# Three edits to a one-core fp32 transformer pass: order of the first loads, the pool stage's halves one tile later, and one masked product per scan step

## The reference

```python
for layer in range(DEPTH):
    f = swiglu(rms_norm(h, g[0]), ffn_w_gate[layer, 0], ffn_w_up[layer, 0], ffn_w_down[layer, 0])
    h = h + 0.5 * rms_norm(f, g[1])
    hm = rms_norm(h, g[2])
    if layer < N_A_LAYERS:
        mix = pool_mixer(hm, ...)      # u = h @ w_in; windowed mean of u minus u; group matmul; w_out
    else:
        mix = dilated_mixer(hm, ...)
    h = h + rms_norm(mix, g[3])
    ...                                # second swiglu of the layer
# second block, per layer: HGRN2 scan (both directions), global, differential and window attention
S_t = diag(f_t) S_{t-1} + k_t^T v_t ;  o_t = q_t S_t      # gla_chunk_scan, per head, 64 x 64 state
```

## Time and profile before

| | |
|---|---|
| median of 3 runs | 3438.83 us (3436.82 to 3443.32) |
| the profiled execution | 3444.33 us, its span 3442.5 us |
| instructions | 55261 |
| PE busy | 3204.3 us, 93% of the span |
| DVE / ACT / POOL busy | 43% / 34% / 40% |
| mean granted clock of TensorE | 0.959 |

### The profile page before, as it was taken

How to read it: one execution, slowest core, us unless ns; L and a number is a source line. 1 busy time by engine, 2 the same in 40 slices (tenths; PEclk the granted TensorE clock), 3 DMA queues, 4 the chain that set the end, 5 groups by cost and what they waited for, 6 DMA issues and landing times.

```text
span 3442.5 us, 55261 instructions
## 1 busy us (share of the span) xinstructions
PE 3204.3 (93%) x20656; PEld 2418.0 (70%) x20656; DVE 1473.6 (43%) x3123; ACT 1156.0 (34%) x1979; POOL 1381.4 (40%) x2212
## 2 busy tenths in 40 slices
PE   6999999999999999999999999888989888789888
PEld 5888777787787786777688787666666666556555
DVE  3232454132632235444422236664564345664654
ACT  3222333222421223111322235443434334445444
POOL 3555464454554453333355463331431123323323
PEclk9999999999999999999999999888989999989989
DMA  3222222424334332111133432000000112001011
GB/s 130 97 97 98 86 86 78 139 98 141 106 103 135 133 109 69 56 62 61 57 111 126 140 105 86 31 16 25 32 26 33 61 43 74 26 26 38 32 44 62
DMA packets 74362, 264.71 MB, mean 77 GB/s; under 512 B 7856, under 2 KB 9136, under 8 KB 73904
## 3 DMA queue, kind: packets, MB, share of 16 engines
q1 hardware_dynamic: 67104, 242.25, 21.0%
q10 hardware_dynamic: 7056, 19.69, 1.5%
HBM read 252.47 MB, written 7.34 MB: 75 GB/s over the span
## 4 chain that ended last, share of the span: by engine, by line
PE 82%; DVE 10%; ACT 3%; issue 3%; POOL 0%; DMA 0%; ACTq 0%; DVEq 0%; POOLq 0%
PE ps L1414 28%; PE ps L1443 17%; PE ps L1419 14%; PE ps L1407 3%; PE ps L1937 3%; PE ps L1960 2%; PE ps L1910 2%; PE ps L1517 1%; PE ps L1804 1%; DVE tb L2627 1%; PE ps L1743 1%; PE ps L1990 1%; PE ps L1498 1%; DVE work L2430 1%; PE ps L1824 1%
## 5 line engine op out<-in xcount | busy, mean ns | idle before, releaser
L923 POOL TENSOR_TENSOR wl<-raw,wh 128x256 fp32r<-128x256 f32 x1640 | 1209.9, 769 | 1879.0 <-ACT wh L1020 1248.9
L1042 ACT ACTIVATE wh<-raw 128x1024 fp32r<-128x1024 f32 x224 | 237.6, 1061 | 976.3 <-PE ps L1419 842.6
L1414 PE MATMUL ps<-xh,wh 128*128 128x512 f32 x1392 | 542.7, 390 | 1.7 <-ACT wh L1020 1.7
L1414 PE MATMUL ps<-xl,wh 128*128 128x512 f32 x1392 | 541.6, 389 | 0.0
L1419 PE MATMUL ps<-xh,wl 128*128 128x512 f32 x1392 | 344.3, 389 | 1.2 <-POOL wl L923 1.0
L1020 ACT ACTIVATE wh<-raw 128x1024 fp32r<-128x1024 f32 x186 | 196.7, 1058 | 429.5 <-PE ps L1443 250.7
L1414 PEld LDWEIGHTS ps<-xh,wh 128*128 128x128 f32 x1392 | 261.3, 188 | 59.9 <-ACT wh L1020 3.3
L1419 PEld LDWEIGHTS ps<-xh,wl 128*128 128x128 f32 x1392 | 261.0, 188 | 56.7 <-POOL wl L923 2.7
L1414 PEld LDWEIGHTS ps<-xl,wh 128*128 128x128 f32 x1392 | 261.3, 188 | 53.9
L1414 PE MATMUL ps<-ah,wh 128*128 128x512 f32 x748 | 296.5, 396 | 0.5 <-DVE al L2239 0.5
L1443 PE MATMUL ps<-xh,wh 128*128 128x512 f32 x856 | 278.3, 389 | 19.0 <-issue 7.6
(11 more groups left out here) (374 smaller groups left out, 4934.9 us busy)
## 6 DMA issues: line engine op xcount, KB each, us to landing
raw<-wts_dram SPq DMA_DIRECT2D x458, 512.0 KB, 3.5
spilled_dram<-hc ACTq DMA_DIRECT2D x1, 3072.0 KB, 8.7
hc<-spilled_dram ACTq DMA_DIRECT2D x1, 3072.0 KB, 10.1
tb<-tab_dram ACTq DMA_DIRECT2D x5, 512.0 KB, 3.7
hc<-x_dram ACTq DMA_DIRECT2D x8, 256.0 KB, 9.4
spilled_dram<-hc ACTq DMA_DIRECT2D x1, 2048.0 KB, 7.3
hc<-spilled_dram ACTq DMA_DIRECT2D x1, 2048.0 KB, 8.3
out_dram<-hc SPq DMA_DIRECT2D x8, 256.0 KB, 2.1
```

The source lines that it names most:

```text
L923: ins = pool.tensor_tensor(wl[:, n % SPLIT, piece], raw[:, LOADED[n] % RAW, piece], wh[:, n % SPLIT, piece].bitcast(F32), ALU.subtract)
L1042: act.activation(wh[:, n % SPLIT, :], raw[:, at % RAW, :], ACT.Copy).then_inc(hi_done, 1)
L1414: pe.matmul(out_, wh[:, s, k * P:(k + 1) * P], x_(k, at), start=first, stop=False)
```

## The change

**Opening.** SP now issues the loads in this order: weight tile 0, `x` piece 0, weight tile 1, `x` pieces 2 to 7, weight tiles 2 and 3, constants, masks, levels, context. ACT issues the parameters and `x` piece 1. Each piece of `x` has its own semaphore. The matrix of ones is made by DVE instead of being loaded. PE begins tile 0 when tile 0 has its remainder, and waits for that of tile 1 where tile 1 begins. PE's wait for the constants and for Silu of `cc` stands behind the first two tiles; ACT computes that Silu behind the first gate's Silu; DVE copies the masks before its first gate tile.

**Pool stage.** ACT rounds, and POOL subtracts, the mean of tile n-1 in the step of tile n, and those of the last two tiles both in the step of tile 7 (`pool_parts_after`).

**Scan.** The masks of the near and the far products are one table of 320 columns, and `take` is one product over 2 x 320 columns, the sum and the key copy. The three copies and the clearing of `far` are gone. The state of both heads lies in the same 64 columns, so that `update` has one instruction for it in place of two.

```diff
-NLEV = 2 * NLOW * BLK
+NSCAN = NLOW * BLK + P
+NLEV = 2 * NSCAN
...
-    c["ones"] = np.ones((P, P))
...
-    levels = np.stack([np.stack(low, 1), np.stack(back, 1)], 1).reshape(P, -1).astype(np.float32)
+    far = np.zeros((P, P))
+    for l, s0, q0 in ((6, 0, 64), (5, 0, 32), (5, 64, 96)):
+        far[s0:s0 + (1 << l), q0:q0 + (1 << l)] = 1.0
+    ways = [np.concatenate([np.stack(v, 1).reshape(P, -1), f], 1) for v, f in ((low, far), (back, far.T))]
+    levels = np.concatenate(ways, 1).astype(np.float32)
...
-        const_in, cond_in = sem("const_in"), sem("cond_in")
+        gains_in, ones_ready, const_in, cond_in = sem("gains_in"), sem("ones_ready"), sem("const_in"), sem("cond_in")
+        x_in = [sem(f"x_in{k}") for k in range(KC)]
...
-        far = area(SX + 240, 2 * P).rearrange("p (h t) -> p h t", h=2)
-        lowp = area(SX + 240 + 2 * P, 2 * NLOW * BLK).rearrange("p (h l t) -> p h l t", h=2, l=NLOW)
+        scanned = area(SX + 240, 2 * NSCAN).rearrange("p (h n) -> p h n", h=2)
+        far = scanned[:, :, NLOW * BLK:]
+        lowp = scanned[:, :, 0:NLOW * BLK].rearrange("p h (l t) -> p h t l", l=NLOW)
...
+        def pool_parts_after(number):
+            ins = [m for what, m in POOL_TILES if what == "in"]
+            last = len(ins) - 1
+            return ins[last - 1:] if number == last else ins[number - 1:number] if 0 < number < last else []
...
-            for n in range(RAW):
+            def first_raw(n):
                 sp.dma_start(raw[:, n, :], wts[n * P:(n + 1) * P, :]).then_inc(raw_in[n], 16)
+            def first_x(k):
+                sp.dma_start(hc[:, k, 0:SEQ], x[k * P:(k + 1) * P, :]).then_inc(x_in[k], 16)
+            first_raw(0)
+            first_x(0)
+            first_raw(1)
+            for k in range(2, KC):
+                first_x(k)
+            first_raw(2)
+            first_raw(3)
+            for dst, src in ((cn[:, :], con), (area(0, NMASK), masks), (area(NMASK, NLEV), levels)):
+                sp.dma_start(dst, src).then_inc(const_in, 16)
+            sp.dma_start(hc[:, :, SEQ:TOK], ctx_in).then_inc(cond_in, 16)
...
-                    late = []
-                    for what, m in POOL_TILES:
+                    def part_low(k):
+                        pool.wait_ge(part_hi, c.take("part") + 1)
+                        pool.tensor_tensor(alk(k), tt[:, k % 2, :], ahk(k).bitcast(F32), ALU.subtract).then_inc(a_ready, 1)
+                    for number in range(len(POOL_TILES)):
...
-                        for k in late:
-                            pool.wait_ge(part_hi, c.take("part") + 1)
-                            pool.tensor_tensor(alk(k), tt[:, k % 2, :], ahk(k).bitcast(F32), ALU.subtract).then_inc(a_ready, 1)
-                        late = [m] if what == "in" else []
+                        for k in pool_parts_after(number):
+                            part_low(k)
...
+                    if (name, *at) == ("ffn", 0, 0):
+                        act.wait_ge(x_in[k], 16)
+                        if k == 0:
+                            act.wait_ge(gains_in, 16)
...
+                        if (layer, i) == (0, 0) and number == 0 and j == 0:
+                            give(act.activation(col("cc", 0, 2 * KC), col("cc", 0, 2 * KC), ACT.Silu), a2p, "a2p")
...
+                def part_high(k):
+                    act.wait_ge(part_ready, c.take("part") + 1)
+                    act.activation(ahk(k), tt[:, k % 2, :], ACT.Copy).then_inc(part_hi, 1)
...
-                    if what == "in":
-                        act.wait_ge(part_ready, c.take("part") + 1)
-                        act.activation(ahk(m), tt[:, m % 2, :], ACT.Copy).then_inc(part_hi, 1)
-                    else:
+                    for k in pool_parts_after(number):
+                        part_high(k)
+                    if what == "group":
...
-            for dst, src in ((cn[:], con), (pr[:], par), (area(0, NMASK), masks), (area(NMASK, NLEV), levels)):
-                act.dma_start(dst, src).then_inc(const_in, 16)
-            for k in range(KC):
-                act.dma_start(hc[:, k, 0:SEQ], x[k * P:(k + 1) * P, :]).then_inc(const_in, 16)
-            act.dma_start(hc[:, :, SEQ:TOK], ctx_in).then_inc(cond_in, 16)
-            act.wait_ge(const_in, CONST_LOADS * 16)
-            give(act.activation(col("cc", 0, 2 * KC), col("cc", 0, 2 * KC), ACT.Silu), a2p, "a2p")
+            act.dma_start(pr[:], par).then_inc(gains_in, 16)
+            act.dma_start(hc[:, 1, 0:SEQ], x[P:2 * P, :]).then_inc(x_in[1], 16)
...
-                pe.wait_ge(lo_done, n0 + 2)
+                pe.wait_ge(lo_done, n0 + 1)
...
+                    if j == 1 and k == 0:
+                        pe.wait_ge(lo_done, n0 + 2)
...
+                if (layer, i) == (0, 0):
+                    pe.wait_ge(const_in, CONST_LOADS * 16)
+                    get(a2p, "a2p")
...
-                        pe.matmul(out_banks[:, h, :], qi[s % 2][r, :], state[r, h * HEAD:(h + 1) * HEAD], start=True, stop=False, skip_group_check=True)
+                        pe.matmul(out_banks[:, h, :], qi[s % 2][r, :], state[r, :], start=True, stop=False, skip_group_check=True)
...
-            pe.wait_ge(const_in, CONST_LOADS * 16)
-            get(a2p, "a2p")
+            pe.wait_ge(ones_ready, 1)
...
+                    dve.wait_ge(const_in, CONST_LOADS * 16)
+                    own(dve.tensor_copy(mk[:, :], area(0, NMASK)))
+                    own(dve.tensor_copy(lev.rearrange("p a n -> p (a n)"), area(NMASK, NLEV)))
...
-                    pv = ps[:, 6:8, 0:NLOW * BLK].rearrange("p h (l t) -> p h l t", l=NLOW)
-                    own(dve.tensor_tensor(lowp, pv, lev[:, way].unsqueeze(1).to_broadcast([P, 2, NLOW, BLK]), ALU.mult))
-                    dve.tensor_reduce(lows, lowp.rearrange("p h l t -> p h t l"), AX.X, ALU.add).then_inc(near_ready, 1)
-                    both = ps[:, 6:8, NLOW * BLK:NLOW * BLK + P]
-                    for rows, cols, l in far_products(way):
-                        ins = dve.tensor_copy(far[rows, :, cols], both[rows, :, cols])
-                    ins.then_inc(far_ready, 1)
+                    dve.tensor_tensor(scanned, ps[:, 6:8, 0:NSCAN], lev[:, way].unsqueeze(1).to_broadcast([P, 2, NSCAN]), ALU.mult).then_inc(far_ready, 1)
+                    dve.wait_ge(far_ready, n + 1)
+                    dve.tensor_reduce(lows, lowp, AX.X, ALU.add).then_inc(near_ready, 1)
...
-                for h in range(2):
-                    r = slice(HEAD * h, HEAD * (h + 1))
-                    sh = state[r, h * HEAD:(h + 1) * HEAD]
-                    ins = dve.scalar_tensor_tensor(sh, sh, sd[r, s % 4:s % 4 + 1], state_bank[r, h * HEAD:(h + 1) * HEAD], ALU.mult, ALU.add)
-                ins.then_inc(state_ready, 1)
+                dve.scalar_tensor_tensor(state, state, sd[:, s % 4:s % 4 + 1], state_bank, ALU.mult, ALU.add).then_inc(state_ready, 1)
...
-                    own(dve.memset(far, 0.0))
...
-            dve.wait_ge(const_in, CONST_LOADS * 16)
-            own(dve.tensor_copy(mk[:, :], area(0, NMASK)))
-            own(dve.tensor_copy(lev.rearrange("p a l t -> p (a l t)"), area(NMASK, NLEV)))
...
-            own(dve.tensor_copy(ones_r[:, :], ones))
-            for layer in range(DEPTH):
-                for i in (1, 5):
-                    g = col("norm", (layer * 6 + i) * KC, KC)
-                    own(dve.tensor_scalar(g, g, 0.5, None, ALU.mult))
+            own(dve.memset(sq[:, 0, 0:P], 1.0))
+            dve.tensor_copy(ones_r[:, :], sq[:, 0, 0:P]).then_inc(ones_ready, 1)
+            dve.wait_ge(ones_ready, 1)
...
+            dve.wait_ge(gains_in, 16)
+            for layer in range(DEPTH):
+                for i in (1, 5):
+                    g = col("norm", (layer * 6 + i) * KC, KC)
+                    own(dve.tensor_scalar(g, g, 0.5, None, ALU.mult))
...
```

More of the change, by code:

```diff
@@ L564 @@
 WORK = 9728
-CONST_LOADS = 4 + KC
+CONST_LOADS = 3
 MAGIC = 1.5 * 2.0 ** 23
```

13 lines of the change are left out of this document (7 added, 6 removed).

## The result

The changed kernel takes 3394.45 us (median of 4 runs, 3393.35 to 3396.05), beside 3440.92 (4 runs, 3436.82 to 3443.32) for the kernel before in the same job: a ratio of 0.9867, 95% interval 0.9849 to 0.9884, or 46 us. The profiled execution took 3396.05, against 3444.33: 48.3 us less.

What follows compares the result with a forecast made beforehand. PE, busy 93% of the span, was taken as the bound. Terms -15.1, -3.5, -13 and -2 sum to -33.6: profiled 3444.3 to 3410.7, or 3405 us against the median; own range 3396 to 3413, 8 in 10 within 3392 to 3419.

Steps and rivals of the forecast that it cites:

- the rival in which all of DVE's saved time counts: Whole kernel: nearly all 31 us saved on DVE lie on the path and the clock gains too, 3390; chance 0.14.
- the clock: Mixers: shorter waits leave fewer PE stretches at 1.2 GHz, taken as -2 us, between 0 and -8.
- Term 1: Opening: PE's first product at about 10 us instead of 26.5, partly given back; -15.1 us, bounds -12.5 to -16.5.
- The stall: After the first two tiles: PE waits for ACT's Silu of `cc`, +1.3 us.
- Term 2: Pool stage: earlier rounding and an earlier last `al` shorten PE's wait; -3.5 us, bounds -1 to -5.
- DVE's chain: Pool stage: DVE's means slow by 0.9 us as POOL's work moves forward, leaving the last `al` 3.9 us earlier.
- Term 3: Mixers' scan: shorter `take`, one update instruction and no clearing of `far`; -13 us, bounds -5 to -20.
- 28 x 0.41 = 11.5: Scan: `take` gets 0.41 us shorter on average, and PE waits for it 28 times; -11.5 us.
- The first rival: Scan: PE waits for ACT or its own order instead, so the scan gives 5 us, not 15: 3415; chance 0.17.
- The state's update, -3.5: Scan: `update` loses one of two 0.28 us instructions; -3.5 us taken, between -2.0 and -7.7.

Runs made afterwards that it cites:

- the pair of runs with copies ahead and behind: Changed kernel plus three 128x69 SBUF copies on DVE per full step, before the key copy (3406.23 us) or after it (3393.89 us).
- the kernel with the better opening: Changed kernel with PE's wait for constants and Silu of `cc`, and DVE's mask copies, moved after the first gate part, and `xh` between weight roundings: 3387.48 us.
- the run with the SBUF copies: Changed kernel plus three back-to-back 128x69 SBUF copies on DVE between the near sum and the key copy in each full step: 3406.23 us.
- the other two traces of the same mixers: Kernel before with only the new opening (3425.24 us), and kernel before with only the pool stage's list change (3434.86 us).
- the product alone: Kernel before with the masked wide product and without its three copies, the state's update still in two instructions: 3409.48 us.
- the added copy: Changed kernel plus one 128x69 SBUF copy on DVE ahead of the state's update in each of the 48 steps: 3392.16 us.

## Why the prediction was right, and where it was not

The forecast's mechanism held in all three places, and 3394.45 lies in the range of 3392 to 3419. It is 10.6 us below the 3405 named, just outside the forecast's own range (3396 to 3413), and between it and the rival in which all of DVE's saved time counts (3390). The wide range reaches down to 3392 because of this rival, which the pair of runs with copies ahead and behind refutes. What brought the time down there was in large part the clock, for which I had -2, so that the time lies inside the range is in part luck. The sum of the terms was -33.6, measured -48.3 from profile to profile. The profiled executions stood 5.5 above the median before, as I had it, and 1.6 after, so 3.9 us of that gap do not reach the medians.

**Term 1, the opening: -15.1 predicted, -12.9 measured.** The mechanism was right and two sizes were off. The first product came at 11.54, in the 9 to 12 named, but not at the 10 taken. The second weight tile came 0.7 us later than I had assumed. Then `xl`, the last to come as I had said, was costed at 0.71, but the first three took 3.61 us beside a busy POOL, where a later one took 0.75. The stall was 2.04 in place of 1.3, because the mask copies, costed at +0.1, took 1.86 us and were not hidden by rstd; ACT stood 0.59 us for what came behind them. Before, they ran while POOL was idle, and the one of the same shape took half as long:

```profile
16.73 0.49 DVE L2745 CAST mk<-work 128x640 bf16<-128x640 f32 x1 [16.73 <-DMA hc<-x_dram]
17.26 0.36 DVE L2746 CAST lev<-work 128x384 bf16<-128x384 f32 x1
```

The stall and the late start together are what the kernel with the better opening won back (4.3 us there).

**Term 2, the pool stage: -3.5 predicted, about -2.3 measured.** Two steps failed. The last `al` does follow its mean as I said, 2.0 us behind it where it was 6.7 (468.29 to 475.03):

```profile
459.02 0.17 DVE L2303 TENSOR_TENSOR work<-work,tb 128x16 f32<-128x16 f32 x1
...
459.93 1.28 POOL L1010 TENSOR_TENSOR al<-work,ah 128x512 fp32r<-128x512 f32 x1 [2.42 <-ACT ah L1168]
```

But DVE's chain grew by 3.6 us, not 0.9, so that from the first scaling of the stage the last `al` comes only 1.2 us earlier, not 3.9. At that product PE's lead has grown by 0.9 us; the other 1.4 come right behind it, where the kernel before ran 3.4 us at the lower clock level (476.4 to 479.8); the changed one has its stretch at that level earlier, from 450.7 to 454.1. I had taken POOL's cost as an average, 0.45 us of DVE for each microsecond that POOL is busy, and let 2 us of POOL's work move into the stretch. One instruction of 1.3 us moved in. The rest of the cost is that POOL's work now lies beside DVE's additions where it had left gaps, which the average can't show: the 20 additions went from 966 to 1319 ns. The 0.77 us that I read as an addition beside an idle POOL was not one, since POOL has rows at that time; alone it takes 0.69. POOL's busy time in the window rose by 4.5 us (36.41 to 40.88) for the one instruction more, since its own pieces are slowed as well:

```profile
443.58 0.72 POOL L950 TENSOR_TENSOR wl<-raw,wh 128x256 fp32r<-128x256 f32 x1
...
446.32 1.17 POOL L950 TENSOR_TENSOR wl<-raw,wh 128x256 fp32r<-128x256 f32 x1
```

So each side waits for the other, and what that costs is not a fixed share of POOL's busy time. The Trainium skill (page "SBUF — State Buffer", section "Who interferes with whom") says that a VectorE instruction with two SBUF inputs contends with a GpSimd instruction that reads SBUF. The trace agrees, with 0.69 and 1.11 us on the one side and 0.72 and 1.17 on the other.

And the wait ahead of the group product was not in the term. It grew by 1.3 us, and does so in the kernel with the pool list alone too.

**Term 3, the scan: -13 predicted; the mixers gave -32.6 with the clock.** The step "28 x 0.41 = 11.5" was nearly right: `take` became 0.54 shorter, since the copies cost more with their gaps than I took, and the waits fell by 13.7. The product at 0.82 was the predicted 0.84. That these waits count about once is what the run with the SBUF copies shows: 13.4 us of waits put back cost 12 by the medians, though its trace has only 7.7 us more of idle time. The first rival, that the waits move, was there at most in small. PE's idle time fell by 9.0 where this wait fell by 13.7 (14 and 15 beside the other two traces of the same mixers), and the waits for ACT (13.1, now 12.7) and for the operands (11.6, now 12.2) stayed as they were the earlier trace rows, so no single one took over.

The step that failed is the last of the sum: "I take -2 between 0 and -8" for the clock. PE's busy time from the mixers on fell by 23.5 us with the matmuls unchanged, from one trace to the other. By the timed runs it is less: the clock rose from about 0.961 to 0.9655, and within one kernel executions that differ by 0.001 in mean clock differ by about 2 us (the kernel before: 0.963 at spans of about 3434, 0.959 at 3442). That makes about 9 us of the medians' 46, at or beyond the bound of -8 and not near the -2 taken. The state's update, -3.5, measured 5.6 us between the kernels with the product alone and with the whole scan, which is not clear of noise, and 10 to 12 us alone. In that run the wait for the key copy was as long as before and the clock higher, 0.964 in place of 0.961 in its timed runs, so by the same price some 6 us of its gain are clock.

**What stays open.** Put back to the old length of `take`, the changed kernel took 3406. The kernel before took 3440. Of those 34 us the opening and the pool stage are 15, the update 6 to 10. Some 9 to 13 are left, with equal waits and a clock of 0.961 against 0.966. The medians of the single parts (15.0, 5.4, 36.4) also add up to 10 us more than the whole, which is about as much as their intervals allow. It may be that the kernel before loses some microseconds of clock which it gets back with any of the edits; that is not shown. What in the placing of the waits decides the clock no run here separates. Whether the update's length costs anything by itself is open as well, since the added copy lengthened it too little.

## What to carry to other kernels

Where one engine waits for another in each step of a chain, ask what stands between the producer and the signal that it waits for: copies that lengthened the way there by 0.54 us in each of 40 steps cost 12 us, behind the signal nothing, and moving a sum of 0.86 us behind it won 9 more. Price an idle gap of TensorE with the clock behind it as a term of its own, and with wide bounds: here 13 us of waits put back cost 12, and 8 more cost 17 to 18. Take a split into busy and idle time from more than one trace, since three of the same mixers differ by 16 us of busy time. When work of GpSimd is moved, do not price it by an average over the stretch, but ask which VectorE instructions with SBUF inputs will start beside it that had its gaps before, and look for small copies that land beside it, such as the masks.

## What the runs showed of the hardware

A VectorE addition of two SBUF inputs, 128x512, took 0.69 us alone, 1.11 or 1.75 beside POOL's subtractions: 966 ns on average beside a POOL busy for 80% of the window, and 1319 beside one busy for 83% but with its work placed elsewhere. POOL's pieces of 128x256 took 0.72 us, and mostly 1.17 beside such additions. Casts of 128x640 from FP32 to BF16 took 0.94 and 0.92 us beside POOL, 0.49 without it. A product of 640 columns of PSUM with a BF16 mask took 823 ns, where 384 columns took 0.57 us: 1.0 ns for each column more. Copies of 128x69 in SBUF have a mean of 263 ns, but three lengthened the way by only 0.54 us when they followed each other, and by 0.77 when each waited: the mean of one holds the overlap with its neighbours, which the busy total, 24.8 us for 120, counts once.
